# Loading a mixture-of-experts layer's up weights in two transfers of 4 MB instead of four of 2 MB

## The reference, cut to what matters

```
for e in range(32):
    hid = xt @ w_up[e] + b_up[e]              # w_up[e]: 1024 x 2048, 8 MB
    x_glu = minimum(hid[:, :1024], 7)
    x_lin = clip(hid[:, 1024:], -7, 7)
    act = x_glu * sigmoid(1.702 * x_glu) * (x_lin + 1)
    y = act @ w_down[e] + b_down[e]           # w_down[e]: 1024 x 1024, 4 MB
    out = out + gates[:, e:e+1] * y           # the gate is 0 for tokens that did not choose e
```

## Time and profile before

| | us |
|---|---|
| median of 3 runs | 1312.49 |
| the 3 runs | 1309.84 to 1315.05 |
| the profiled execution, its own time | 1309.69 |
| its span, first to last instruction | 1307.9 |

### The profile page before, as it was taken

The page is one execution under the profiler, slowest core; times in us unless marked ns, Lnnn a source line. Parts: engine busy times, 40 slices in busy tenths (PEclk is TensorE's granted clock), DMA queues, the critical chain, the costliest instruction groups (busy, mean ns, idle before and its releaser), DMA issues.

```text
span 1307.9 us, 15366 instructions
## 1 busy us (share of the span) xinstructions
PE 1219.1 (93%) x5850; PEld 540.0 (41%) x5851; DVE 381.8 (29%) x785; ACT 191.6 (15%) x376; POOL 62.1 (5%) x87
## 2 busy tenths in 40 slices
PE   2899999979999999999999999999999999999996
PEld 1788735554343344333333333333344343333332
DVE  1854345643111321111222111111221112221114
ACT  2100146311100111000111010000111001101101
POOL 2230025100000000000000000000000000000000
PEclk9899999979999999999999999999999999999998
DMA  9974387435499999999999999999599999999690
GB/s 379 350 169 169 125 290 192 163 129 206 179 381 430 427 430 427 429 428 428 428 428 429 428 430 427 429 428 428 236 416 429 428 427 429 428 429 429 268 384 33
DMA packets 54757, 455.46 MB, mean 348 GB/s; under 512 B 22496, under 2 KB 22520, under 8 KB 26032
## 3 DMA queue, kind: packets, MB, share of 16 engines
q1 hardware_dynamic: 52128, 449.86, 84.3%
q10 hardware_dynamic: 2176, 3.75, 0.9%
q0 software_dynamic: 432, 1.57, 0.3%
HBM read 454.11 MB, written 1.05 MB: 348 GB/s over the span
## 4 chain that ended last, share of the span: by engine, by line
PE 55%; DMA 35%; DVE 4%; issue 2%; ACTq 2%; ACT 1%; POOL 0%; DVEq 0%; SPq 0%; POOLq 0%
DMA ring<-in_moe_w_up 35%; PE bank L1181 23%; PE bank L1228 9%; PE bank L998 8%; PE bank L1013 2%; PE bank L1071 2%; PE bank L956 2%; PE bank L1167 2%; PE bank L1021 1%; PE bank L1034 1%; ACTq L450 1%; DVE hT_mem L887 1%; DVE v_mem L893 1%; DVE v_mem L894 1%; PE bank L1115 1%
## 5 line engine op out<-in xcount | busy, mean ns | idle before, releaser
L1181 PE MATMUL bank<-ring,v_mem 128*64 128x512 f32 x2240 | 495.6, 594 | 28.7 <-DMA ring<-in_moe_w_up 28.3
L1181 PEld LDWEIGHTS bank<-ring,v_mem 128*64 128x64 f32 x2240 | 181.2, 137 | 334.7 <-issue 274.5
L1228 PE MATMUL bank<-ring,v_mem 128*64 128x512 f32 x1120 | 248.1, 594 | 1.5
L893 DVE TENSOR_SCALAR v_mem<-bank 128x512 f32<-128x512 f32 x35 | 24.2, 692 | 718.7 <-PE bank L1191 718.7
L1228 PEld LDWEIGHTS bank<-ring,v_mem 128*64 128x64 f32 x1120 | 92.6, 137 | 132.7 <-issue 132.5
L569 ACT ACTIVATE v_mem<-v_mem 128x512 f32<-128x512 f32 x35 | 22.1, 630 | 537.8 <-DVE v_mem L893 537.8
L887 DVE TENSOR_TENSOR hT_mem<-hT_mem,bank 128x512 f32<-128x512 f32 x140 | 89.4, 680 | 8.0 <-PE bank L1167 8.0
L1167 PE MATMUL bank<-v_mem 64*128 64x512 f32 x280 | 78.8, 640 | 3.4 <-ACT v_mem L581 0.8
L1107 PE MATMUL bank<-q_mem,pT_mem 128*64 128x512 f32 x288 | 71.4, 617 | 1.3 <-DVE pT_mem L836 1.3
L368 POOL TENSOR_TENSOR rstd<-ms,neghalf 128x1 f32<-128x1 f32 (+1 forms) x8 | 4.8, 594 | 1077.0 <-DVE ms L617 1077.0
L581 ACT ACTIVATE v_mem<-bank 128x512 f32<-128x512 f32 x35 | 20.9, 597 | 228.6 <-PE bank L1228 228.6
(11 more groups left out here) (215 smaller groups left out, 969.5 us busy)
## 6 DMA issues: line engine op xcount, KB each, us to landing
ring<-in_moe_w_up SPq DMA_DIRECT2D x128, 2048.0 KB, 23.2
ring<-in_moe_w_down SPq DMA_DIRECT2D x64, 2048.0 KB, 20.3
ring<-in_ada_w SPq DMA_DIRECT2D x24, 1024.0 KB, 9.4
ring<-in_na_w_qkv SPq DMA_DIRECT2D x12, 1024.0 KB, 23.6
tokens<-in_na_rpb SPq DMA_DIRECT2D x64, 64.0 KB, 6.3
ring<-in_na_w_o SPq DMA_DIRECT2D x4, 1024.0 KB, 17.6
gain<-in_norm_g POOLq DMA_DIRECT2D x3, 512.0 KB, 5.8
tokens<-in_x ACTq DMA_DIRECT2D x1, 1024.0 KB, 12.2
```

The source lines that it names most:

```text
L893: d.tensor_scalar(glu, bank[0][:, :], LIMIT, None, ALU.min).then_inc(glu_ready, 1)
L1181: last = mm(bank[half][64 * n:64 * n + 64, :], xT[:, k % 4, 64 * (k // 4):64 * (k // 4) + 64], w[:, c0:c0 + HALF], start=k == 0, stop=False)
L1228: last = mm(bank[2][64 * n:64 * n + 64, :], aT[:, j, 64 * half:64 * half + 64], w[:, HALF * n:HALF * n + HALF], start=k == 0, stop=k == KC ...
```

## The change

The up weights of an expert come in two chunks of 4 MB, of four slots each: four neighbouring rows of 2048 numbers in a partition, 32 KB side by side. The down weights stay in two chunks of 2 MB. An expert has 4 chunks instead of 6. TensorE waits for, and gives back, an up chunk at every fourth k instead of at every second. The transposes of the gathered tokens pick columns in steps of 4. The slots of the ring that each byte goes to are the same in number and order.

```diff
-PER, UPS = 6, 4
+PER, UPS = 4, 2
...
+        def chunk_slots(j):
+            return 4 if j < UPS else 2
+        def slots_to(j):
+            return sum(chunk_slots(i) for i in range(j))
         def expert_chunk(j):
-            s = (EXP + 2 * j) % RING
-            return ring[:, s:s + 2, :].rearrange("p s n -> p (s n)")
+            s = (EXP + slots_to(j)) % RING
+            return ring[:, s:s + chunk_slots(j), :].rearrange("p s n -> p (s n)")
...
-            up_2k = w_up[0].rearrange("e (j p k) n -> e j p (k n)", p=P, k=2)
+            up_4k = w_up[0].rearrange("e (j p k) n -> e j p (k n)", p=P, k=4)
...
-                src = (up_2k[bass.ds(e, 1), j] if j < UPS else down_4k[bass.ds(e, 1), j - UPS])
+                src = (up_4k[bass.ds(e, 1), j] if j < UPS else down_4k[bass.ds(e, 1), j - UPS])
...
-                sp.wait_ge(ring_free, EXP - RING + 2 * j + 2)
+                sp.wait_ge(ring_free, EXP - RING + slots_to(j + 1))
...
-                    c0 = 2 * P * (j // 2) + j % 2
-                    last = tr(bank[3][:, P * j:P * j + P], xe[:, c0:c0 + 2 * P - 1:2], ident[:, :])
+                    c0 = j
+                    last = tr(bank[3][:, P * j:P * j + P], xe[:, c0:HALF:4], ident[:, :])
...
-                    if k % 2 == 0:
-                        expert_chunk_here(pe, e, k // 2)
-                    w = expert_chunk(k // 2)[:, 2 * D * (k % 2):2 * D * (k % 2) + 2 * D]
+                    if k % 4 == 0:
+                        expert_chunk_here(pe, e, k // 4)
+                    w = expert_chunk(k // 4)[:, 2 * D * (k % 4):2 * D * (k % 4) + 2 * D]
...
-                    if k % 2 == 1:
+                    if k % 4 == 3:
                         last.then_inc(ring_free, 1)
```

## The result

| us | before | after |
|---|---|---|
| median of 18 runs each | 1313.91 | 1319.18 |
| fastest run | 1309.84 | 1316.19 |
| the profiled execution, its own time | 1309.69 | 1319.74 |
| its span | 1307.9 | 1317.9 |

The ratio is 1.0041, with a 95% interval of 1.0027 to 1.0055.

The account below looks back on a forecast made before the run. Bound by a path alternating between TensorE and weight transfers, switching at pauses after two-block experts; 2.59 + 3.44 + 2.60 + 3.44 - 1.8 = +10.3 us on the median 1312.49 gives 1322.8 us, range 1314 to 1331.

Parts of the forecast that it names:

- paid-back rival: Up transfers reach 433 GB/s, 1.2% faster, so most of the loss returns: +5.4 us, 1317.9, within 0.5%; chance 0.20.
- The pauses after two-block experts: First load after a pause waits for half an up phase, not a quarter: +3.43 us first, +3.44 second, before the gap's saving.
- The last landing with a half phase behind it: After an expert's last up byte 6.87 us of multiplications remain instead of 3.43: +3.44 us at each of two places.
- The third pause: Last expert's later loads stay hidden: second 4 MB lands at 1280.7, wanted at 1285.0, 4.3 us to spare.
- Up transfers of expert 1 in time: Before the first pause, expert 1's second 4 MB lands by 332, block 1's second half starts at 336.6: no loss.
- Transposes in steps of 4: Transposes of gathered tokens at L1115 cost 0; upper bound 0.2 us a block, 1 us in all.
- fewer waits and issues: Two TensorE waits and two SP issues fewer per expert: nothing to gain.
- the transfers' own price: Half the packets of the up loads, about 4 ns each, save 0.06 us an expert over 29 up shares: -1.8 us.
- a gap of 0.84: After the first and second pauses, the queue's dry gap before the first down chunk disappears, saving 0.84 us each.
- The rival on the other side: Larger transfers run faster in the 29 up shares; at 5% more rate -16 us, 1296; chance 0.07.

Follow-up runs that it names:

- free_half: Kernel before, but SyncE issues the up transfers of 2 MB in pairs, each pair once its second slot chunk is used; TensorE waits as before; ratio 1.0037.
- wait_half: Kernel before with its 2 MB up transfers, but TensorE waits for two of them together and gives each back at once as before; ratio 1.0046.
- both_half: Kernel before with 2 MB transfers and 16 KB rows, but with both the paired waits and the paired, later issues; ratio 1.0090.
- rows_32k: Kernel before with 2 MB up transfers, but 16 KB pieces lying 32 KB apart and transposes in steps of 4; ratio 0.9989.
- four_16k: Changed kernel with its 4 MB up transfers, but two 16 KB pieces per partition and transposes in steps of 2; ratio 1.0072 against the kernel before.
- one_8mb: Changed kernel with the 8 MB of up weights in one transfer, one wait and one give-back a block; 1594.52 us, ratio 1.2131 against the kernel before.
- mix_2411: Kernel before with up transfers of 2, 4, 1 and 1 MB in the layout of before; ratio 1.0059.

## Why the prediction was right, and which terms were mis-sized

The sign, the path and the place of every loss were right, and 1319.18 is inside the range. The size was not: +10.3 was forecast, with +7 to +14 as the likely band, +5.3 is the difference of the medians and +5.95 that of the traces. The result fell out of that band, and inside the range only because the range took in the paid-back rival. The forecast said slower by more than 0.5%, with a chance of 0.73; it is 0.4%, which stood there with a chance of 0.20.

*Right.* The pauses after two-block experts as the only places where a late give-back counts: +3.44 at the first (forecast +3.43), alone in free_half. The last landing with a half phase behind it: +3.44 at two places, alone in wait_half. That both add up: both_half. The third pause is hidden: its restart is 13.4 us later in absolute time (1256.09 against 1242.66), 9.4 of it the change, and no wait for weights appears in the last 65 us. Up transfers of expert 1 in time: no loss before the first pause. Transposes in steps of 4 at nothing (rows_32k; in the changed kernel 922.70 to 929.34, which holds them, is 6.64 again), and fewer waits and issues at nothing (TensorE's three stretches leave no room for them).

*Mis-sized: "the transfers' own price".* The prediction took 4 ns a packet from a window of mixed small rows, and so 0.06 us an expert, -1.8 in all. It is 9 to 10 ns a piece, 0.15 an expert: -4.2 (2.82 + 1.40 between four_16k and after). The window from 10 to 18 us was a poor row for it: two queues run there at once (304 and 299 packets), with pieces of other sizes, and a few GB/s in 8 us had to carry the whole price.

*Mis-sized: "a gap of 0.84".* Taken from issue times alone. What a dry queue costs is best read in the traffic. Windows behind the first restart, of the kernel before and then of the kernel after:

```profile
360.45:390.45 30.00, 29.81 (x142) 11.98 (x140) 6.34 (x14) 3.19 (x6) 0.00 (x0) 1.00 0.97 389
380.45:384.45 4.00, 4.00 (x22) 1.64 (x20) 0.00 (x0) 0.28 (x1) 0.00 (x0) 1.00 0.88 303
```

```profile
367.93:397.93 30.00, 29.81 (x142) 11.97 (x140) 6.33 (x14) 3.19 (x6) 0.00 (x0) 1.00 0.98 411
387.93:391.93 4.00, 4.00 (x22) 1.64 (x20) 0.00 (x0) 0.60 (x1) 0.00 (x0) 1.00 0.96 410
```

Against the steady 428 GB/s, 389 over 30 us is a loss of 2.7 us and 411 one of 1.2. The latter holds some longer pieces; four_16k, with the pieces of before, moves 409 to 410 behind its restarts, a loss of 1.3. So a restart with late down transfers costs 1.4 to 1.5 us more, where I had 0.84. The stretches say -4.96 - 2.84 = -7.8 for both pieces and restarts, of which -4.2 is pieces and -3.6 the two restarts (-2.14 and -1.44 in four_16k; forecast: -1.7). The window explains the second; the 0.7 left of the first is no more than one profile resolves. (With transfers of 2 MB, free_half and both_half, the same two stretches gave back 1.61 and 1.13, and 1.46 and 1.00.)

*The rivals.* "Mostly paid back" came nearest in size, +5.4, and its mechanism, a slightly better rate, is half of what happened: the rate of the up transfers rose by 0.8% (0.15 of 19.58 us), not by 1.2%, and the restarts gave the rest. The rival on the other side named the right mechanism (a price per row that halves), but it needed far more than was there: +2.1% of the up rate by the prediction's own sum, against the 0.8%. The fixed part of 2 us that the Trainium skill gives a transfer ("DMA: Bandwidth & Descriptors", section "Anatomy of one DMA", told there for transfers issued by GpSimd) is nowhere in a queue that is never empty: with two transfers fewer, four_16k lands at the same interval.

No arrangement tried is measurably faster than the kernel before. By the measured prices (10 ns a piece and engine, the rule on landings, the give-backs) there is little to win by cutting alone. Up transfers of 2, 2, 2, 1 and 1 MB, for example, were not run; the rule gives 2 x (1.97 - 3.43) = -2.9 us for them and the pieces of 8 KB +2.3, an estimate of -0.6. Computing the two blocks of an expert side by side on each chunk, which would remove the pauses, was not tried.

## What to carry to other kernels

When a stream of weights is the bound, waiting for larger chunks costs nothing in the steady stretches but counts wherever the stream starts again and wherever its end is waited for: take the latest of landing plus remaining work over all chunks, and the time to the first give-back, at each such place, and count the places. Set against it the price per contiguous piece times the pieces of the whole stream; here 6 us of a loss of 13.8 were left, because longer pieces and a fuller queue at the restarts gave back 7.8. Check also how much is left in the queue when a chunk comes free: once that is shorter than the chunk's computation, the cost jumps from a few us to one per expert (1594.52 us with 8 MB).

## What the runs showed of the hardware

- A contiguous piece costs an engine 9 to 10 ns beside its bytes, between 8 and 32 KB, and the number of transfers that the pieces are split over costs nothing in a full queue: 29.68, 29.37 and 29.22 us for 12 MB with 8, 16 and 32 KB pieces of up weights, and 29.37 for 16 KB pieces in transfers of 2 MB or of 4 MB.
- During 8.46 us without work TensorE's granted clock fell (one_8mb: 0.78 in the mean of 8 us), it was 0.50 in the first 2 us of work behind and 1.00 again 4 us on. Waits of 1.70 us in the middle of the up phase (after) were followed by 32 instructions at the old pace, 7.1 us. In mix_2411 waits of 1.92 us were followed by 48 instructions in 12.22 us with the clock at 0.50 in some blocks, and in 10.52 us in others; what decides between them is not shown.
- The granted clock in the first 300 us differs between executions of the same work (0.66 or 1.00 at 170 to 180 us), and moves the start of block 0 by 3 to 6 us, as much as the effect studied. The stretch from block 0 on does not carry it: block 0 to the first restart takes 64.97 us in after and four_16k, with the low clock before it, and in both_half and free_half, without.
